# PEER trunk on one core: prompt activations with the tokens on the partitions, gates split in two parts, one-hot rows in three buffers

## What is computed

```python
def block(xb):                                    # 128 tokens
    q = (xb @ w_q).reshape(PEER_BLOCK, H_P, 2, D_HALF)
    s = einsum('thcd,hcnd->thcn', q, sub_keys)    # 8 heads x 2 x 128 keys
    sv, si = top_k(s, 16)
    cand = sv[:, :, 0, :, None] + sv[:, :, 1, None, :]
    best, pos = top_k(cand, 16)                   # 8 x 16 experts per token
    g = softmax(best, axis=-1)
    act = gelu(einsum('thkd,td->thk', u_tab[idx], xb))
    return einsum('thk,thkd->td', g * act, v_tab[idx])
```

## Time and profile before

| | us |
|---|---|
| median of 3 runs | 5468.78 |
| profiled execution | 5471.31 |
| its span | 5469.6 |
| TensorE busy | 5148.1 |
| VectorE busy | 2765.6 |
| ScalarE busy | 1416.1 |
| GpSimd busy | 1494.2 |

### The profile page before, as it was taken

One profiled execution on the slowest core, in us unless ns is written; L12 is line 12 of the kernel. 1 busy time (PEld: TensorE's weight loads), 2 busy tenths in 40 slices (PEclk: granted clock), 3 DMA queues, 4 the chain that ended last, 5 costly groups with the idle time before them and its releaser, 6 DMA issues.

```text
span 5469.6 us, 70249 instructions
## 1 busy us (share of the span) xinstructions
PE 5148.1 (94%) x30167; PEld 4571.9 (84%) x30167; DVE 2765.6 (51%) x4785; ACT 1416.1 (26%) x1532; POOL 1494.2 (27%) x839
## 2 busy tenths in 40 slices
PE   6999779999999989999899999899999999999998
PEld 3767679999999978888666678889999999878886
DVE  2162669914444146666555541389524442166666
ACT  0110022223444222222222222112234443222222
POOL 0020222332222265542011110123322222455531
PEclk7969999999999999999799999999999999999999
DMA  7141022334444478886210011113334444588873
GB/s 293 63 165 59 20 77 82 121 118 153 156 158 154 167 255 300 304 302 258 84 38 33 31 44 46 46 60 112 119 135 155 157 155 153 195 312 302 294 295 142
DMA packets 295263, 835.85 MB, mean 153 GB/s; under 512 B 23923, under 2 KB 157299, under 8 KB 242727
## 3 DMA queue, kind: packets, MB, share of 16 engines
q1 hardware_dynamic: 91680, 520.91, 25.8%
q10 hardware_dynamic: 158216, 176.07, 9.4%
q0 software_dynamic: 45056, 134.38, 7.2%
HBM read 674.40 MB, written 156.80 MB: 152 GB/s over the span
## 4 chain that ended last, share of the span: by engine, by line
PE 89%; DVE 6%; POOL 2%; DMA 1%; ACT 1%; issue 1%; SPq 0%; DVEq 0%; ACTq 0%; POOLq 0%
PE PS L584 20%; PE PS L586 20%; PE PS L585 20%; PE PS L635 4%; PE PS L716 3%; PE PS L429 3%; PE PS L829 3%; PE PS L807 3%; PE PS L489 3%; PE PS L791 2%; POOL A L1847 1%; PE PS L576 1%; DVE EP L1348 1%; DMA ring<-in_w_mod 1%; PE PS L713 1%
## 5 line engine op out<-in xcount | busy, mean ns | idle before, releaser
L584 PE MATMUL PS<-hH,wH 128*128 128x320 f32 x4608 | 1439.2, 312 | 29.5 <-DVE hL L1116 28.4
L585 PE MATMUL PS<-hL,wH 128*128 128x320 f32 x4608 | 1425.0, 309 | 0.0
L586 PE MATMUL PS<-hH,wL 128*128 128x320 f32 x4608 | 1425.0, 309 | 0.0
L1836 POOL TENSOR_TENSOR wL<-raw,wH 128x2048 fp32r<-128x2048 f32 x144 | 669.1, 4647 | 1659.4 <-ACT wH L1570 1659.4
L584 PEld LDWEIGHTS PS<-hH,wH 128*128 128x128 f32 x4608 | 867.0, 188 | 30.7 <-issue 29.2
L585 PEld LDWEIGHTS PS<-hL,wH 128*128 128x128 f32 x4608 | 867.2, 188 | 0.0
L586 PEld LDWEIGHTS PS<-hH,wL 128*128 128x128 f32 x4608 | 866.2, 188 | 0.0
L1570 ACT ACTIVATE wH<-raw 128x2048 fp32r<-128x2048 f32 x272 | 520.5, 1914 | 1111.4 <-PE PS L586 1052.0
L586 PE MATMUL PS<-wH,WL 128*128 128x512 f32 x2048 | 803.8, 392 | 0.0
L1223 DVE TENSOR_TENSOR wL<-raw,wH 128x2048 fp32r<-128x2048 f32 x128 | 293.4, 2292 | 463.3 <-ACT wH L1570 463.3
L1855 POOL DMA_INDIRECT ubuf<-in_v,idxV x256 | 356.3, 1392 | 582.3 <-DVE acc L1235 539.6
(11 more groups left out here) (331 smaller groups left out, 6571.9 us busy)
## 6 DMA issues: line engine op xcount, KB each, us to landing
raw<-in_u SPq DMA_DIRECT2D x128, 1024.0 KB, 4.8
raw<-in_v SPq DMA_DIRECT2D x128, 1024.0 KB, 4.9
expert_acts<-abuf ACTq DMA_DIRECT2D x128, 640.0 KB, 2.9
expert_gates<-wide ACTq DMA_DIRECT2D x64, 1024.0 KB, 5.1
wide<-expert_acts SPq DMA_DIRECT2D x64, 1024.0 KB, 5.6
ring<-in_w_mod SPq DMA_DIRECT2D x48, 1024.0 KB, 8.7
wide<-expert_gates SPq DMA_DIRECT2D x16, 2048.0 KB, 11.8
gb<-expert_gates SPq DMA_DIRECT2D x16, 2048.0 KB, 12.0
```

What stands on the lines that cost most here:

```text
L584: nc.tensor.matmul(out, lhsH, rhsH, start=start, stop=False)
L585: nc.tensor.matmul(out, lhsH, rhsL, start=False, stop=False)
L586: return nc.tensor.matmul(out, lhsL, rhsH, start=False, stop=stop)
L1836: G.tensor_tensor(wL[:, n % NSPLIT, :], raw[:, n % NRAW, :], wH[:, n % NSPLIT, :].bitcast(f32), ALU.subtract).then_inc(lo_u, 1)
```

## The change

- The sample's activations keep the weights stationary, with all 512 tokens as one stream of 512 columns, into one bank per block (0 and 1 alternate): 8 x 3 matmuls per block.
- The prompt's activations are turned: after each odd block, the 128 prompt tokens are stationary and the 256 expert columns of both blocks stream, 8 x 3 matmuls into bank 2, with a gelu of their own and a store every fourth pair of blocks to a new DRAM tensor `prompt_acts`, one row per token. `expert_acts` keeps the 512 sample tokens only. The fetch index becomes token x 16384 + expert, with less arithmetic.
- Gates are split as the other operands are: the high part in gP[:, 0], the rest in gP[:, 1], made by three operations after the transposes. The rows of ones and of gates become `f32r`; the second operand of a build is a pair of rows, so that one matmul of 256 columns gives the table of the high part and of the rest. A build comes in two halves of four tokens (`build(q, c)`), both into banks 3 and 4: the first half in the middle of the block, the second at its end, after the prompt's products in odd blocks.
- ScalarE copies the high table to `gst` (`gate_half`, counted in `g_high`), VectorE adds the rest to it in place (`gates_out`, counted in `g_evac`).
- `hots` now has two comparisons and two multiplications, three buffers, and is made two groups ahead: groups 0 and 1 before the loop, group q+2 in two parts between the two adds of group q.
- The store of 16 tokens' gates is issued in the block after the odd one.

The core of the diff:

```diff
-                def act_block(b):
+                def act_block(b, build_group):
-                    done(feature_major_split(slot, b % 2, b % 2), ("a", l, b))
+                    for half in range(2):
+                        for k in range(4 * half, 4 * half + 4):
+                            w = slice(k * SLICE + (b % 2) * P, k * SLICE + (b % 2 + 1) * P)
+                            last = split_products(PS[:, b % 2, :], wH[:, slot, w], wL[:, slot, w], hH[:, k, P:T], hL[:, k, P:T],
+                                                  k == 0, k == KD - 1)
+                        if half == 0 and build_group is not None:
+                            build(build_group, 0)
+                    done(last, ("a", l, b))
+                    if b % 2 == 1:
+                        if l * 64 + b // 2 >= 1:
+                            pe.wait_ge(act0_gelu, l * 64 + b // 2)
+                        for k in range(KD):
+                            w = slice(k * SLICE, (k + 1) * SLICE)
+                            last = split_products(PS[:, 2, 0:SLICE], hH[:, k, 0:P], hL[:, k, 0:P], wH[:, slot, w], wL[:, slot, w],
+                                                  k == 0, k == KD - 1)
+                        done(last, ("a0", l, b // 2))
+                    if build_group is not None:
+                        build(build_group, 1)
-                def build(q):
+                def build(q, c):
+                    if c == 0:
+                        pe.wait_ge(hot_ready, l * NGRP + q + 1)
+                    if q or c:
+                        pe.wait_ge(g_evac, 2 * (l * NGRP + q) + c)
+                    for tk in range(4):
+                        last = nc.tensor.matmul(PS[:, 3 + tk // 2, (tk % 2) * 2 * P:(tk % 2 + 1) * 2 * P].rearrange("p (c j) -> p c j", c=2),
+                                                hots_[q % 3][:, 0, 4 * c + tk, :], hots_[q % 3][:, 1:3, 4 * c + tk, :], start=True, stop=True)
+                link(V.tensor_copy(gH[:], gP[:, 0, :]))
+                link(V.tensor_tensor(gP[:, 1, :], gP[:, 0, :], gH[:].bitcast(f32), ALU.subtract))
+                link(V.tensor_copy(gP[:, 0, :], gH[:].bitcast(f32)))
...
+                        link(V.tensor_tensor(hots_[q % 3][:, 1], one, bc(gP[:, 0, ts], N_KEYS), ALU.mult))
+                        V.tensor_tensor(hots_[q % 3][:, 2], one, bc(gP[:, 1, ts], N_KEYS), ALU.mult).then_inc(hot_ready, 1)
...
+                def gates_out(q, c):
+                    ve.wait_ge(g_high, 2 * (l * NGRP + q) + c + 1)
+                    first = (q % 2) * 8 + 4 * c
+                    out = gst[:, q // 2 % 2, :, first:first + 4].rearrange("p i t -> p t i")
+                    V.tensor_tensor(out, out, gates_[:, 1], ALU.add).then_inc(g_evac, 1)
+                def gate_half(q, c):
+                    s, first = q // 2 % 2, (q % 2) * 8 + 4 * c
+                    act.wait_ge(products, at["g", l, q, c])
+                    if q % 2 == 0 and c == 0 and l * 32 + q // 2 >= 2:
+                        act.wait_ge(g_stored[s], 16 * (l * 16 + q // 4))
+                    S.activation(gst[:, s, :, first:first + 4].rearrange("p i t -> p t i"), gates_[:, 0], ACT.Copy).then_inc(g_high, 1)
```

More of the change, by code:

```diff
@@ L249, in trunk @@
     WL1 = sb("WL1", [P, JV, DEC], f32r, scope=pv)
-    sb("v_pad", [P, 82 * KB], scope=pv)
+    sb("v_pad", [P, 80 * KB], scope=pv)
+    acc0 = sb("acc0", [P, D], scope=pv)
+    ubuf0 = sb("ubuf0", [P, D], scope=pv)
     WL0 = sb("WL0", [P, JV, DEC], f32r, scope=pv)
-    acc0 = sb("acc0", [P, D], scope=pv)
-    ubuf = sb("ubuf", [P, NGAT, D], scope=pv)
+    ubuf1 = sb("ubuf1", [P, NGAT - 1, D], scope=pv)
+    ubuf = [ubuf0[:]] + [ubuf1[:, i, :] for i in range(NGAT - 1)]
     pv.close()
@@ L1202, in hots @@
-                    V.tensor_tensor(hots_[:, q % 2, 1], hots_[:, q % 2, 1], bc(gT[:, ts], N_KEYS), ALU.mult).then_inc(hot_ready, 1)
-                for q in range(NGRP):
-                    hots(q)
+                    one = hots_[q % 3][:, 2].bitcast(f32)
+                    if half == 0:
+                        if q >= 3:
+                            ve.wait_ge(products, at["g", l, q - 3, 1])
+                        do(V.tensor_tensor(hots_[q % 3][:, 0], io, bc(hkT[:, 0, ts], N_KEYS), ALU.is_equal))
+                        do(V.tensor_tensor(hots_[q % 3][:, 2], io, bc(hkT[:, 1, ts], N_KEYS), ALU.is_equal))
+                    else:
+                        settle()
+                        link(V.tensor_tensor(hots_[q % 3][:, 1], one, bc(gP[:, 0, ts], N_KEYS), ALU.mult))
+                        V.tensor_tensor(hots_[q % 3][:, 2], one, bc(gP[:, 1, ts], N_KEYS), ALU.mult).then_inc(hot_ready, 1)
@@ new lines, in gates_out @@
+                def gates_out(q, c):
[3 more added lines that the diff above has]
+                    V.tensor_tensor(out, out, gates_[:, 1], ALU.add).then_inc(g_evac, 1)
+                for q in range(2):
+                    hots(q, 0)
+                    hots(q, 1)
+                for q in range(NGRP):
+                    gates_out(q, 0)
+                    if q < NGRP - 2:
+                        hots(q + 2, 0)
+                    gates_out(q, 1)
+                    if q < NGRP - 2:
+                        hots(q + 2, 1)
@@ L1607, in peer @@
                         act.wait_ge(a_stored[pr % 2], 16 * (l * 32 + pr // 2))
-                    S.activation(abuf[:, pr % 2, half, :].rearrange("p (a t) -> p a t", a=2), PS[:, 2 * half:2 * half + 2, 0:HT], ACT.Gelu).then_inc(act_gelu, 1)
+                    S.activation(abuf[:, pr % 2, half, :], PS[:, half, :], ACT.Gelu).then_inc(act_gelu, 1)
                     if half == 1:
@@ L1842, in peer @@
                     pool.wait_ge(a_stored[half], 16 * 32 * (l + 1))
-                pool.wait_ge(products, at["a", l, N_KEYS - 1])
+                    pool.wait_ge(a0_stored[half], 16 * 8 * (l + 1))
+                pool.wait_ge(products, at["a0", l, 63])
                 pool.wait_ge(hot_ready, NGRP * (l + 1))
@@ L1959, in gate_load @@
                         elif b == 1:
-                            sp.wait_ge(products, at["a", l, N_KEYS - 1])
+                            sp.wait_ge(products, at["a0", l, 63])
                         else:
```

124 lines of the change are left out of this document (59 added, 65 removed).

## The result

The changed kernel takes 5339.12 us (median of 4 runs, 5337.52 to 5341.90) against 5468.38 (4 runs, 5466.64 to 5473.68): a ratio of 0.9764, 95% interval 0.9751 to 0.9778. In five later runs, beside the kernel before, it was 0.9765.

What follows compares the result with a forecast made beforehand. TensorE was taken as the bound, busy 94% of the span. 129 us saved on products and builds, less 33 for waits and 19 for the start, gave 77; from 5471.3, less 2.5 for the median, 5392 us, range 5345 to 5455.

Steps and rivals of the forecast that it cites:

- 64 pairs without groups: Expert-activation stage, pairs of blocks without gate builds: fewer, wider products save 0.17 us per pair, 11 us in all.
- 64 pairs with groups, without waits: Expert-activation stage, pairs with gate builds: from 17.64 to 15.80 us each if nothing new waits, 118 us in all.
- waits for the adds: TensorE's builds wait for VectorE's adds, 3G - 2.96 us per pair if G is over 0.99: 0.52 each, 33 us lost.
- start of the groups: First groups of each layer: TensorE waits 4.3, then 2.9 and 0.3 us, plus 2 for lower clock; 19 us lost.
- G: Length of VectorE's add of 512 gate elements with the 64-byte step, paid once: taken as 1.16 us.
- T: Timetable of a pair with groups: the moment when TensorE has issued the odd block's second half build.
- rival 3: Prompt products and gate builds: 256 columns cost what 320 do, 0.1466 us, bound by the weight load; 5491 us, chance 0.05.
- Costed at nothing: ScalarE's work, later gate store, GpSimd's subtraction, SyncE's loads, index arithmetic and the switch to the values: no cost, values ±3 us.
- rival 1: VectorE's adds: the step costs nothing, G up to 0.99, no steady wait; 5359 us, chance 0.17.
- 2: Rival, VectorE's adds: read and write each pay the step, G 1.63, 124 us of waits; 5483 us, chance 0.08.
- 4: Rival, VectorE's adds: read and write overlap partly, G 1.35 to 1.56, waits 70 to 110 us; 5429 to 5469, chance 0.12.
- 5: Rival, one-hot rows: the third buffer does not keep groups two ahead; no chance of its own.

Runs made afterwards that it cites:

- no step: Changed kernel with each half group's gates copied and added contiguously, without the step of 64 bytes; 5329.77 us, ratio 0.9755.
- early transposes: Changed kernel with the transposes of indices and gates one block earlier and the exponentials two blocks earlier; 5328.69 us, ratio 0.9752.
- late store: Changed kernel with the gates' store issued in the odd block itself, behind its group's last add, as before the change; 5405.38 us, ratio 0.9891.
- longer adds: Changed kernel with a copy out of PSUM ahead of every VectorE add: 5367.16 us with 64 elements, 5448.07 us with 512.
- two buffers: Changed kernel with two buffers for the one-hot rows in place of three, each group made one ahead in place of two; 5749.08 us.
- combined kernel: Changed kernel with transposes a block earlier, VectorE's group work reordered and the gathered rows weighed one step later; 5302.27 us, ratio 0.9700.

## Why the prediction was right and wrong

The forecast's timetable of who waits for whom held; its terms, above all the waits for the adds, were priced too high. The sum again, with what each term measured, both layers (plus is a gain):

| term | forecast | measured | from |
|---|---|---|---|
| 64 pairs without groups | 11 | 19 | 14.07 to 13.78 |
| 64 pairs with groups, without waits | 118 | 123 | 17.65 to 15.73 (no step) |
| waits for the adds | -33 | -10 | no step against changed |
| start of the groups | -19 | -14 | early transposes against changed |
| values and the switch to them | 0 | 3 | stages |
| sum | 77 | 121 | stages: 122 |

- **The waits for the adds** are the step that failed: the term was taken as 33 us and measured 10. The mechanism held: three adds in a row (each us more in an add costs 2.9 per pair), the step paid once, the limit near the forecast's. G was 1.10, not 1.16, which by the forecast's own 3G - 2.96 leaves 0.34 us per pair; 0.16 was measured. The rest lies in counting operations by length. Where one VectorE operation follows another its start is 0.1 us earlier than the end of the one ahead, and the forecast used such spacings for multiplications and comparisons, but not for the add itself. With 1.01 us for the first two adds, behind which another operation starts, and 1.10 for the third, the same formula gives 3.12 - 2.96 = 0.16. That this fits so well is partly luck, since other terms of it were off in both directions: the add began at T+1.27, not T+1.43, and TensorE came to the odd block's first build at T+9.16, not T+9.24.
- **Products.** 0.119 for 256 columns was right (0.120), and rival 3 (0.147) falls. For 512 columns the value stage's 439 records in 100 us give 0.228; the forecast rounded it up to 0.230 for missing records, and the activation stage has 0.227. 0.003 x 48 is 0.14 us per pair, 18 us over all pairs; the 256-column products (0.120, not 0.119) and the builds (1.95 us per pair, not 1.90) take some 6 of that back, which leaves about the 13 by which the first two rows of the table are better. (The prediction's T+15.32 for the odd block's second build adds up to 15.34; nothing hangs on it.)
- **The start**: the first wait was right (4.05 against 4.3); the second (2.9) and the 2 us of lower clock were added, while the slow clock itself covered the second wait. 7 us per layer, not 9.5.
- **Costed at nothing** were right: the late store, SyncE, GpSimd. A gate store now takes 6.5 us to land, not 5.1, far from the limit of 11. The wait at the values moved as said and cost little more (15.1 us in one piece, 14.2 in two before).
- **Rivals.** 1 said that the step costs nothing, 5359; it costs 10 us, so it falls as stated, but the time came out on its side. 2 and 4 needed G over 1.35 and fall. 5 falls: the third buffer keeps ahead, and without it the kernel would be slower than before.
- **The range** was too narrow below. The prediction itself gave 5330 as rival 1's lower end, with cheaper products, and yet put the bound at 5345; that products, waits and start could all be better at once (44 us) was not in it. With the stages' 122 us alone the time would be 5346, just inside; the last step out of the range goes with the unchanged first half, 7 us shorter in the profiled run, and is chance.

## What to carry over

Where operations of one engine stand in a row, take start-to-start distances for all of them, the new one too: of the 23 us by which a 33 us term was overstated here, half came from lengths in place of distances, half from an add priced 0.06 us too high that counts three times. Where a chain has just no slack, ask for each link what moves it: the store's place alone was worth 66 us, the third buffer over 400. And when several terms are each rounded to the cautious side, let the range have them all wrong together.

## What the hardware showed beside that

- Waits of TensorE had different prices. Those of 0.5 to 0.9 us (late store, longer adds) cost themselves, at a clock of 1.00. With two buffers some of the waits of 1.9 to 2.2 us were followed by 3.3 us at 1.2 GHz and others were not, and a pair lost 6.5 us for 3.85 of waiting. What makes the difference is not shown.
- The price of a product (us) against its columns is flat, then steep: 0.112 at 128, 0.120 at 256, 0.147 at 320, 0.227 at 512. So 256 columns cost hardly more than 128, and over the other three points the price about follows the columns.
- With VectorE's add and ScalarE's copy stepping by 64 bytes, the stretch from the odd block's first build to its second took 6.16 us, without the step 6.08: half of the step's 0.16 us per pair sits there. The combined kernel keeps the step, with VectorE's work in another order, and takes 6.08 too; so what costs there is how late the add is, not the step itself.
